# A 64x64 block inversion in a scan: odd heads' intermediate in the other partition half, two banks for its products

## The reference, cut to what matters

```python
def step(S, inp):
    r_t, w_t, k_t, v_t, kk_t, a_t = inp
    sa = -jnp.einsum('nhvk,nhk->nhv', S, kk_t)
    S = S * w_t[:, :, None, :] + sa[..., None] * (kk_t * a_t)[:, :, None, :] + v_t[..., None] * k_t[:, :, None, :]
    return S, jnp.einsum('nhvk,nhk->nhv', S, r_t)
```

## Time and profile before

| | us |
|---|---|
| median of 3 runs | 4755.96 (4754.23 to 4760.57) |
| the profiled execution: time | 4752.73 |
| its span | 4750.7 |
| scan `rwkv()`, from its first products to the last (about 2887 to 3357) | 470 |

### The profile page before, as it was taken

How to read it: one execution, slowest core, us unless ns; L and a number is a source line. 1 busy time by engine, 2 the same in 40 slices (tenths; PEclk the granted TensorE clock), 3 DMA queues, 4 the chain that set the end, 5 groups by cost and what they waited for, 6 DMA issues and landing times. The chain is left out here.

```text
span 4750.7 us, 68994 instructions
## 1 busy us (share of the span) xinstructions
PE 4214.0 (89%) x28006; PEld 2452.3 (52%) x28006; DVE 1979.8 (42%) x3941; ACT 1351.4 (28%) x3136; POOL 517.9 (11%) x535
## 2 busy tenths in 40 slices
PE   5999889999998999999997766888698799999994
PEld 2455456654444666455546545777585344433431
DVE  1464256612563564325205665666346222222224
ACT  2124445511144554112113443333032111111110
POOL 0000000000000000000000002222002422322220
PEclk9999989999999999999997877888898899999997
DMA  5122340041222303412011012000304578999995
GB/s 191 55 77 62 89 137 18 13 150 51 90 81 85 122 18 121 159 59 97 26 63 48 2 29 87 3 3 3 116 1 155 225 252 283 327 310 335 335 330 157
DMA packets 194517, 565.70 MB, mean 119 GB/s; under 512 B 24385, under 2 KB 105906, under 8 KB 180754
## 3 DMA queue, kind: packets, MB, share of 16 engines
q1 hardware_dynamic: 157778, 441.90, 25.8%
q0 software_dynamic: 36416, 119.29, 9.1%
HBM read 437.02 MB, written 124.11 MB: 118 GB/s over the span
## 5 line engine op out<-in xcount | busy, mean ns | idle before, releaser
L729 PE MATMUL banks<-arena 128*128 128x512 f32 (+1 forms) x2928 | 1123.3, 541 | 9.4 <-ACT arena L584 5.7
L729 PEld LDWEIGHTS banks<-arena 128*128 128x128 f32 x2928 | 556.0, 191 | 536.8 <-issue 499.2
L3248 PE MATMUL banks<-arena 128*32 128x512 f32 (+2 forms) x2896 | 561.6, 595 | 4.2 <-DMA arena<-in_experts 3.3
L1242 PE MATMUL banks<-arena 128*128 128x256 f32 (+1 forms) x1152 | 376.6, 481 | 18.5 <-DMA arena<-y_d 14.4
L3248 PEld LDWEIGHTS banks<-arena 128*32 128x32 f32 (+2 forms) x2896 | 198.5, 130 | 358.3 <-issue 354.5
L1448 PE MATMUL banks<-arena 96*128 96x512 f32 (+1 forms) x800 | 331.7, 550 | 42.2 <-DMA arena<-k_d 35.2
L1499 DVE TENSOR_REDUCE arena<-banks 128x1 f32<-128x512 f32 (+1 forms) x400 | 226.3, 592 | 262.7 <-PE banks L1448 262.7
L1242 PEld LDWEIGHTS banks<-arena 128*128 128x128 f32 x1152 | 222.0, 194 | 164.6 <-issue 144.9
L3267 PE MATMUL banks<-arena 128*32 128x512 f32 (+2 forms) x1448 | 286.4, 595 | 1.7 <-DVE arena L3297 1.2
L3332 ACT ACTIVATE arena<-banks 128x256 f32<-128x256 f32 x79 | 30.4, 385 | 781.9 <-PE banks L3248 781.9
L3215 POOL DMA_INDIRECT r_d<-arena x125 | 181.5, 1452 | 639.2 <-DVE arena L3297 516.0
(11 more groups left out here) (500 smaller groups left out, 5674.7 us busy)
## 6 DMA issues: line engine op xcount, KB each, us to landing
arena<-in_experts SPq DMA_DIRECT2D x64, 3072.0 KB, 12.8
arena<-in_ada_w SPq DMA_DIRECT2D x12, 2048.0 KB, 7.8
arena<-in_w_in SPq DMA_DIRECT2D x19, 1024.0 KB, 5.9
arena<-in_w_mod SPq DMA_DIRECT2D x8, 2048.0 KB, 17.3
arena<-in_w_in SPq DMA_DIRECT2D x7, 2048.0 KB, 8.5
arena<-in_w_out SPq DMA_DIRECT2D x6, 2048.0 KB, 11.4
arena<-in_tokens SPq DMA_DIRECT2D x4, 2048.0 KB, 17.6
arena<-in_w_mod SPq DMA_DIRECT2D x8, 1024.0 KB, 5.2
```

The lines of the kernel that those rows point to most:

```text
L729: i = e.matmul(self.out_of(n), lhs, rhs, start=k == 0, stop=k == KT - 1)
L1242: i = e.matmul(bank(n % 4)[:, 0:nn], w[:, q, :], H[:, q, t0:t0 + nn], start=q == 0, stop=q == KT - 1)
L3248: op = e.matmul(ABK[(q - q0) % 2][rows, :], xT[(q - q0) % 2][:, P * k:P * k + P][:, rows], weights[:, i % SLOTS, 512 * k:512 * k + 512], s ...
```

## The change

For odd heads X is written to the other partition half: the weights and the moving input are in the half of the chunk, the output in the other. With it the transposed factor that meets XX (TN of odd heads) has to lie in the other half as well; it is made there by 4 more calls in the first gram group (L2382 of the new kernel), and masked with it (the second L2465 takes 128x384 in place of 128x256, wherever the first group is concerned). The product TN' XX of odd heads then crosses back. Products that stay in their half ("straight", `same`) go to the item's first bank, those that cross (`cross`) to its second; both count as taken together (`xo`, `tto`). The order of calls is now by pairs of heads: per pair two straight and two crossing calls of TN' XX, then four straight calls of XX' TN. The number of calls per level is the same. TTN holds T and TN in the order T even, TN even, TN odd, T odd; VectorE's subtraction and ScalarE's copy keep their sizes, and read across the two banks. x1 moves from behind tt of level 0 to behind X of level 1, and its copy from behind the copy of X 0 to ahead of the copy of X 1. A fourth, empty use of the banks keeps their turn. The constants grow by 256 columns (two mask tables); a small table of the attention (`krb`) moves for that.

```diff
-    put("lv1", np.concatenate([levels["lvu", 1], levels["lvl", 1], levels["lvu", 1]], 1))
-    put("rm", np.concatenate([half(r < c), half(r > c), half(r < c)], 1))
+    put("lv1", np.concatenate([levels[name, 1] for name in ("lvu", "lvl", "lvl", "lvu", "lvu", "lvl")], 1))
+    put("rm", np.concatenate([half(r < c), half(r > c)] * 2, 1))
...
-            self.krb = reg(CB + 11 * PW + 1056, 320).rearrange("p (j n) -> p j n", j=NT)
...
+            self.krb = reg(3136 + 3 * 2184, 320).rearrange("p (j n) -> p j n", j=NT)
...
-                self.AB, self.BQ = al(512), al(768)
-                self.AN = self.AB[:, 256:512]
+                self.AB, self.BQ = al(640), al(768)
+                self.AN = self.AB[:, 128:640].rearrange("p (q n) -> p q n", q=4)[:, 0:4:3, :].rearrange("p q (g n) -> p q g n", g=2)
...
-                self.TT_, self.TN = self.TTN[:, 0:256], self.TTN[:, 256:512]
+                self.both = ps[:, 1024 * i:1024 * i + 1024]
...
-                        give("x", n, s_), give("tt", n, s_)
-                        if s_ == 2:
-                            give("x1", n)
-                    give("wt", n, 0), give("wt", n, 1), give("ub", n)
+                        give("x", n, s_), give("xo", n, s_), give("tt", n, s_), give("tto", n, s_)
+                    give("wt", n, 0), give("wt", n, 1), give("ub", n), give("none", n)
+
+            def tt(self, h):
+
+                return self.TTN[:, 384 * (h % 2) + 64 * (h // 2):384 * (h % 2) + 64 * (h // 2) + 64]
+
+            def tn(self, h):
+
+                return self.TTN[:, 128 + 128 * (h % 2) + 64 * (h // 2):192 + 128 * (h % 2) + 64 * (h // 2)]
+
+            def x(self, a, h):
+
+                return a[:, 128 * (h % 2) + 64 * (h // 2):128 * (h % 2) + 64 * (h // 2) + 64]
...
-                                o = P * q + 64 * g
+                                o = P * (q + (pa if gi == 0 else 0)) + 64 * g
                                 op = e.matmul(sl.of("gram", n, gi, pa)[half[c], o:o + 64], lhs[half[pa], g, half[c]], rhs[half[pa], g, half[c]], start=True, stop=True)
+                if gi == 0:
+                    for g in range(2):
+                        for c in range(2):
+                            op = e.matmul(sl.of("gram", n, 0, 1)[half[1 - c], 64 * g:64 * g + 64], b.aT[half[1], g, half[c]], b.bT[half[1], g, half[c]], start=True, stop=True)
                 op.then_inc(Tn.hit("gram", n, gi), 1)
...
-                o = sl.of("x", n, s_)
+                same, cross = b.both[:, 0:512], b.both[:, 512:1024]
...
                 sl.free(e, Vn, Sn, "x", n, s_)
+                sl.free(e, Vn, Sn, "xo", n, s_)
...
                 e.wait_ge(*Vn.at("tt", n, li))
                 e.wait_ge(*Gn.at("am", n, li))
-                for h in range(4):
-                    hs_ = slice(64 * h, 64 * h + 64)
-                    for tp in half:
-                        op = e.matmul(o[tp, hs_], AM[tp, hs_], b.TT_[tp, hs_], start=True, stop=True)
+                for g in range(2):
+                    for c, tp in enumerate(half):
+                        op = e.matmul(same[tp, 384 + 64 * g:448 + 64 * g], b.x(AM, 2 * g)[tp, :], b.tt(2 * g)[tp, :], start=True, stop=True)
+                    for c, tp in enumerate(half):
+                        op = e.matmul(cross[half[1 - c], 64 * g:64 * g + 64], b.x(AM, 2 * g + 1)[tp, :], b.tt(2 * g + 1)[tp, :], start=True, stop=True)
                 op.then_inc(Tn.hit("x", n, li), 1)
-                yield
-                o = sl.of("tt", n, s_)
-                sl.free(e, Vn, Sn, "tt", n, s_)
-                e.wait_ge(*Sn.at("free", "x", n, s_))
-                for lhs, rhs, c0 in ((b.TN, b.XX, 0), (b.XX, b.TN, 256))[0:2 if s_ < 32 else 1]:
-                    for h in range(4):
-                        hs_ = slice(64 * h, 64 * h + 64)
-                        for tp in half:
-                            op = e.matmul(o[tp, c0 + 64 * h:c0 + 64 * h + 64], lhs[tp, hs_], rhs[tp, hs_], start=True, stop=True)
-                op.then_inc(Tn.hit("tt", n, s_), 1)
-                if s_ == 2:
-                    o = sl.of("x1", n)
-                    sl.free(e, Vn, Sn, "x1", n)
...
+                if s_ == 4:
                     there(e, n)
                     e.wait_ge(*Vn.at("free", "gram", n, 1, 1))
                     for h in range(4):
                         hs_ = slice(64 * h, 64 * h + 64)
                         for tp in half:
...
+                            op = e.matmul(same[tp, hs_], b.BT[tp, hs_], v[tp, hs_], start=True, stop=True)
                     op.then_inc(Tn.hit("x1", n), 1)
+                yield
+                sl.free(e, Vn, Sn, "tt", n, s_)
+                sl.free(e, Vn, Sn, "tto", n, s_)
+                e.wait_ge(*Sn.at("free", "x", n, s_))
+                for g in range(2):
+                    for tp in half:
+                        op = e.matmul(same[tp, 128 + 64 * g:192 + 64 * g], b.tn(2 * g)[tp, :], b.x(b.XX, 2 * g)[tp, :], start=True, stop=True)
+                    for c in range(2):
+                        op = e.matmul(cross[half[c], 64 * g:64 * g + 64], b.tn(2 * g + 1)[half[1 - c], :], b.x(b.XX, 2 * g + 1)[half[1 - c], :], start=True, stop=True)
+                    for h in (2 * g, 2 * g + 1) if s_ < 32 else ():
+                        for tp in half:
+                            o = 256 + 128 * (h % 2) + 64 * g
+                            op = e.matmul(same[tp, o:o + 64], b.x(b.XX, h)[tp, :], b.tn(h)[tp, :], start=True, stop=True)
+                op.then_inc(Tn.hit("tt", n, s_), 1)
                 yield
...
-                w_ = len(grp)
-                dst = (b.AB, b.BQ)[gi][:, 0:256 * w_].rearrange("p (q g two n) -> p two q g n", q=w_, g=2, two=2)
-                o_, nc_ = cat[("rm", "rpf" if f else "rpb")[gi]]
-                o_ = CONST + o_ + (64 if gi == 0 and not f else 0)
-                msk = ar[:, o_:o_ + 64 * w_].rearrange("p (q n) -> p q n", q=w_).unsqueeze(2).broadcast_to([P, w_, 2, 64])
                 e.wait_ge(*Tn.at("gram", n, gi))
                 for pa in range(2):
-                    e.tensor_tensor(dst[:, pa], sl.of("gram", n, gi, pa)[:, 0:P * w_].rearrange("p (q g n) -> p q g n", q=w_, g=2), msk, ALU.mult).then_inc(Vn.hit("free", "gram", n, gi, pa), 1)
+                    w_ = len(grp) if gi else 2 + pa
+                    o_, nc_ = cat[("rm", "rpf" if f else "rpb")[gi]]
+                    o_ = CONST + o_ + (64 if gi == 0 and f == pa else 0)
+                    if gi:
+                        dst = b.BQ[:, 0:256 * w_].rearrange("p (q g two n) -> p two q g n", q=w_, g=2, two=2)[:, pa]
+                    else:
+                        dst = b.AB[:, 256 * pa:256 * pa + P * w_].rearrange("p (q g n) -> p q g n", q=w_, g=2)
+                    msk = ar[:, o_:o_ + 64 * w_].rearrange("p (q n) -> p q n", q=w_).unsqueeze(2).broadcast_to([P, w_, 2, 64])
+                    e.tensor_tensor(dst, sl.of("gram", n, gi, pa)[:, 0:P * w_].rearrange("p (q g n) -> p q g n", q=w_, g=2), msk, ALU.mult).then_inc(Vn.hit("free", "gram", n, gi, pa), 1)
                 if gi == 0:
-                    o_ = CONST + cat["lv1"][0] + (0 if f else 64)
-                    lv = ar[:, o_:o_ + 128].rearrange("p (q n) -> p q n", q=2).unsqueeze(2).broadcast_to([P, 2, 4, 64])
+                    o_ = CONST + cat["lv1"][0] + (0 if f else 128)
+                    lv = ar[:, o_:o_ + 256].rearrange("p (q n) -> p q n", q=4).unsqueeze(2).broadcast_to([P, 4, 2, 64])
                     e.wait_ge(*Vn.own())
-                    e.tensor_tensor(b.TTN.rearrange("p (q h n) -> p q h n", q=2, h=4), b.AB.rearrange("p (q h n) -> p q h n", q=2, h=4), lv, ALU.mult).then_inc(Vn.hit(), 1)
...
-                w_ = 512 if s_ < 32 else 256
+                whole = lambda a: a if s_ < 32 else a.rearrange("p (q n) -> p q n", q=4)[:, 0:4:3, :]
                 e.wait_ge(*Tn.at("tt", n, s_))
-                e.tensor_tensor(b.TTN[:, 0:w_], b.TTN[:, 0:w_], sl.of("tt", n, s_)[:, 0:w_], ALU.subtract).then_inc(Vn.hit("free", "tt", n, s_), 1)
+                e.tensor_tensor(whole(b.TTN), whole(b.TTN), whole(b.both[:, 128:640]), ALU.subtract).then_inc(Vn.hit("free", "tt", n, s_), 1)
+                Vn.note("free", "tto", n, s_)
...
-                e.activation(b.XX, sl.of("x", n, s_)[:, 0:256], ACT.Copy).then_inc(Sn.hit("free", "x", n, s_), 1)
-                yield
-                if s_ == 2:
+                if s_ == 4:
                     e.wait_ge(*Tn.at("x1", n))
-                    e.activation(b.X1, sl.of("x1", n)[:, 0:256], ACT.Copy).then_inc(Sn.hit("free", "x1", n), 1)
+                    e.activation(b.X1, b.both[:, 0:256], ACT.Copy).then_inc(Sn.hit("free", "x1", n), 1)
+                e.activation(b.XX, b.both[:, 384:640], ACT.Copy).then_inc(Sn.hit("free", "x", n, s_), 1)
+                Sn.note("free", "xo", n, s_)
...
-                e.tensor_tensor(h64(b.am[li % 2]), h64(b.AN), both4(("lvl" if f else "lvu") + str(LEVELS[li])), ALU.mult).then_inc(Gn.hit("am", n, li), 1)
```

(1 more changed line is left out.)

23 lines of the change are left out of this document (12 added, 11 removed).

## The result

| | median us | lowest to highest | ratio to before, 95% interval |
|---|---|---|---|
| before | 4755.96 | 4749.29 to 4765.5 (9 runs) | 1 |
| after | 4773.94 | 4764.35 to 4777.74 (9 runs) | **1.0032, 1.0021 to 1.0043** |

The account below looks back on a forecast made before the run. No engine is full; a chain in which TensorE, VectorE and ScalarE take turns ending last bounds the scan. Undisturbed periods gain 1.0 us; -28.5 us with the clock as before, +7.5 for the clock: -21, 4735 us, range 4717 to 4755.

Parts of the forecast that it names:

- the deduction for the clock: Steady scan: half of all half-speed spells grow from short to long, one or two new ones ahead of dz; +7.5 us.
- part 3: VectorE from dz to the scaling on which u hangs: shorter X 3, tt 3, X 0 lie beside its work; 0.
- The size of a changed group: TensorE's X and tt groups: each 0.22 us shorter at full clock, ten steps, 2.2 us of TensorE's time per item.
- third rival: Straight and crossing calls do not overlap, so steps give nothing and gram and masking costs remain: +7 us, 4763; 5%.
- Part 1: From ub to VectorE's subtraction of tt 2: tt 1 and tt 2 give -0.22 us each, X 2 gives 0.
- Part 2: VectorE alone, from the subtraction of tt 2 to dz: wider masking +0.13 us, added gram calls hidden.
- Part 4: TensorE from u to the output: shorter groups and moved x1 give -0.7 us (bounds -0.4 and -0.88).
- Part 5: Output, cum, then ScalarE and VectorE in turn until the next ub: 0, x1's copy hidden by exp's wait.
- fourth rival: Idle time around dz starts a second half-speed spell every period, all spells behind ub long: 4761 to 4770; 7%.
- long spell: Half clock for 6.8 us from TensorE's idle time ahead of ub; priced at 2.0 us, against 1.2 for a short one.

Follow-up runs that it names:

- the mended kernels: Idle time filled and GpSimd's masking later, on both kernels; gram count also split on the changed one. Same set: changed 4722.96 us (0.9929), before 4726.17 (0.9935).
- the split count: Changed kernel, but VectorE's first masking waits only for the 16 old gram calls, its second also for the 4 added: 4771.94 us, ratio 1.0033.
- x1_before: Kernel before with only x1 moved behind X 1, and its copy ahead of the copy of X 1: 4763.16 us, ratio 1.0014.
- the masking held back: Changed kernel, but GpSimd's masking waits for ScalarE's copy of X instead of X itself: 4767.24 us, ratio 1.0016.

## Why the prediction was wrong, point by point

Two steps failed. The first and larger is the deduction for the clock: 7.5 us, for longer spells behind ub and "one or two" new ones. The runs showed a second spell in 8 of 13 steady periods and 91 us more half speed in the scan; with the idle time filled in both kernels, the scans were 6.8 us apart in place of 19.7. The second is the zero of part 3, which measured +0.43 us in every period, by the collision with GpSimd.

- **The size of a changed group: right.** X at 0.46 us in place of 0.68. tt with 32 records takes 0.92 where 0.88 was forecast (3283.94 to 3284.86). The cost per quarter of the array, taken from wt and gram, holds for straight and crossing calls too, and with it falls the third rival. The Trainium skill, TensorE: Matmul & The Clock Gate, section "Wait — 56ns, not 53.3ns?", has a floor of about 25 ns between starts; the 48 records of gram 2 in 0.93 us, again in the kernel after, are below it (15 ns each).
- **Part 1: right.** -0.44 forecast, 6.12 to 5.65 is -0.47. X 2 gave nothing there, as taken; in the mended kernels A is 5.2 in place of 5.6.
- **Part 2: too low.** +0.13 for the wider masking, and the added gram calls "hidden". They end 0.12 us behind the subtraction and VectorE waits 0.18 [the timeline above]. B grew by about 0.4 at full clock (3.60 to 4.02, 3.73 to 4.13), of which the split count took 0.15 to 0.2 back; in the mended kernels 0.20 to 0.22 of it is left (3.66 to 3.86 and 3.88), of which 0.13 is the masking. The step to be blamed is a sum of 0.47 + 0.22 + drain that lay within 0.1 us of its cover, from which a zero was taken; I had named its price (0.1), but not as a bound.
- **Part 3: wrong, a missed cost.** "The gains of X 3, tt 3 and X 0 lie beside VectorE's work: 0." It was +0.43. X 0 is also what GpSimd waits for, and a GpSimd instruction that begins first delays VectorE's. All ingredients were in the trace before: GpSimd at 3062.35, released by X, and the scaling at 3062.06, 0.29 us ahead. I followed who waits for TensorE on VectorE and ScalarE, not on GpSimd. The Trainium skill, SBUF — State Buffer, section "Who interferes with whom", tells this very case (a VectorE instruction with two inputs in SBUF against a GpSimd one that reads SBUF: the first takes the port, the other waits); the trace agrees in kind, with 0.86 where a full wait until GpSimd's end (3220.82) plus 0.42 would make 1.00. Spans of GpSimd are rough in a profile, and whether an instruction does its first part while it waits, no run here separates.
- **Part 4: right.** -0.70 forecast, 5.31 to 4.62 is -0.69. x1's move alone gives 0.17 of it (x1_before), and TensorE waits 0.27 us for the copy of X 4 ahead of tt 4 where 0.4 to 0.5 was forecast.
- **Part 5: right in steady periods, wrong ahead of them.** E stayed at 4.89. The cover of x1's copy was named with its price of 0.8, but it was read in a period with output and taken for all. "Estimate 14 x 0.22 = 3 us" for filling and draining had the wrong sign: the two stretches ahead of the first output are 14.1 us longer. In x1_before, where the groups are as before, they are 10.7 us longer. The bare copy is 0.45 us of that in each early period; the rest comes with half speed. With the idle time filled in both kernels 4.4 of the 14.1 are left.
- **The clock: the danger was named, its size was wrong, and this decides.** 7.5 us were taken off for it, and "the longer wait ahead of dz now and then starts a spell of its own (one or two)". It did so in 8 of 13 periods, often enough to put 2.96 us of half speed on D's mean, and the half speed in the scan rose by 91 us. The idle time was forecast at 1.5 + 0.8 us; it came out at 1.17 + 1.24: nothing of X 3's gain reached the first, and the second is longer through the collision. The fourth rival described this course, at 7%: its second spell, its place and its side are right; its claim that all spells behind ub become long is not (A's half speed fell from 4.55 to 3.21). Filling the idle time alone gave 30 us, more than the whole loss.
- **Two slips in the sum, both small.** A long spell was priced at 2.0 us by setting a period of one direction against one of the other; like against like it is 1.8 (A 6.12 to 7.90). And 0.44 + 0.35 + 0.3 in place of 0.22 + 0.22 makes about -1.7 in a period with a long spell, not -1.8. Each is worth 1 to 2 us, and they all but cancel.
- **The observations named to watch:** X 0.46, seen; gram 1 longer by 0.2, seen; wait ahead of ub 1.5, seen; wait ahead of dz at 1.5 and more, not seen (1.17 and 1.30, as before); undisturbed period 21.3, seen only with the masking held back (21.0 to 21.1); granted clock 0.85 to 0.88, it was 0.82; clock low ahead of lo, which was the sign for the fourth rival, seen at 3171.70.

Adding the terms: the period at full clock won 0.3 to 0.5 us in place of 1.0; the second spells took more than that, and a mean period became 0.39 us longer (23.82 to 24.21), 5.1 us in 13. The stretches ahead added 14.1. That makes the 19.7 of the scan but for 0.5 in its tail. Shown by experiment are the part of the clock and, in the stretches, those of the collision, of the gram calls and of the moved x1. Open stays why the spell at the scan's start lasts longer with x1 moved. In the time itself only what the clock takes is clear of noise; the others show in the profiles alone, of which there is one per kernel (two of the mended kernel after).
